# Group D's score matmuls: a head's two sets in turn instead of one after the other

## The reference, cut to what matters

```python
# differential_attention; q, k: (tokens, HEADS=4, 2, DIFF_DH=32)
s = jnp.einsum('bqhtd,bkhtd->bhtqk', q, k).astype(jnp.float32) * scale
p = softmax_f32(s)                              # one softmax for t = 0, one for t = 1
a = (p[:, :, 0] - lam * p[:, :, 1]).astype(v.dtype)
o = jnp.einsum('bhqk,bkhd->bqhd', a, v)
return rmsnorm(o, norm_g) * (1.0 - lam_init)
```

## Time and profile before

| what | value |
|---|---|
| median of 3 runs | 2510.54 us (2506.34 to 2522.1) |
| the profiled execution, first to last instruction | 2507.8 us |
| PE busy with matmuls | 2270.5 us (91%) |
| DVE, ACT, POOL busy | 1359.4 (54%), 790.3 (32%), 493.5 (20%) us |
| group D's attention of layer 0 | 713.4 to 857.8 us |
| group D's attention of layer 1 | 1990.1 to 2104.4 us |

### The profile page before, as it was taken

How to read it: one execution, slowest core, us unless ns; L and a number is a source line. 1 busy time by engine, 2 the same in 40 slices (tenths; PEclk the granted TensorE clock), 3 DMA queues, 4 the chain that set the end, 5 groups by cost and what they waited for, 6 DMA issues and landing times.

```text
span 2507.8 us, 27503 instructions
## 1 busy us (share of the span) xinstructions
PE 2270.5 (91%) x10428; PEld 1820.7 (73%) x10428; DVE 1359.4 (54%) x2448; ACT 790.3 (32%) x1376; POOL 493.5 (20%) x217
## 2 busy tenths in 40 slices
PE   5797989899989779999999989798899997899997
PEld 4675867377866568888888867677466775788886
DVE  5756676244777577676767444554243475411222
ACT  1234242323234442131212233333322344422332
POOL 2200202000200012233222221112001200344442
PEclk9867958555975599999999988777757856899998
DMA  5310302000210013333333211101001100223222
GB/s 202 119 44 16 104 1 94 1 0 1 88 47 1 9 42 134 118 118 118 118 120 126 91 68 34 37 26 61 1 0 39 47 1 17 70 99 101 93 98 70
DMA packets 44770, 161.47 MB, mean 64 GB/s; under 512 B 5344, under 2 KB 5728, under 8 KB 44512
## 3 DMA queue, kind: packets, MB, share of 16 engines
q1 hardware_dynamic: 44640, 159.72, 18.6%
HBM read 157.60 MB, written 2.10 MB: 64 GB/s over the span
## 4 chain that ended last, share of the span: by engine, by line
PE 79%; DVE 11%; ACT 5%; issue 4%; DMA 1%; SPq 0%; POOL 0%; DVEq 0%; ACTq 0%
PE big L1189 64%; PE ob L1189 7%; PE tb L1296 5%; PE tb L1189 3%; DVE pt L908 2%; DVE col L1102 2%; ACT pt L741 1%; DVE pb L952 1%; DMA raw<-w_ada_dram 1%; ACT pb L862 1%; DVE pb L982 1%; DVE h_lo L915 1%; DVE pb L1120 1%; ACT arena L741 1%; DVE z L938 0%
## 5 line engine op out<-in xcount | busy, mean ns | idle before, releaser
L714 POOL TENSOR_TENSOR w_lo<-raw,w_hi 128x1024 fp32r<-128x1024 f32 x182 | 451.8, 2483 | 1244.0 <-ACT w_hi L757 1243.9
L1189 PE MATMUL big<-arena 64*128 64x256 f32 (+4 forms) x1296 | 415.1, 482 | 22.3 <-DVE arena L908 13.4
L1189 PE MATMUL big<-h_hi,w_hi 128*128 128x512 f32 (+1 forms) x1320 | 392.8, 360 | 28.3 <-DVE h_lo L915 27.4
L1189 PE MATMUL big<-h_lo,w_hi 128*128 128x512 f32 (+1 forms) x1320 | 385.5, 354 | 0.0
L1189 PE MATMUL big<-h_hi,w_lo 128*128 128x512 f32 (+1 forms) x1320 | 384.5, 353 | 0.0
L1189 PE MATMUL big<-arena,w_hi 128*128 128x512 f32 (+1 forms) x1536 | 377.1, 354 | 0.0
L1189 PEld LDWEIGHTS big<-arena 64*128 64x128 f32 (+1 forms) x1296 | 278.5, 283 | 124.9 <-issue 71.2
L757 ACT ACTIVATE w_hi<-raw 128x1024 fp32r<-128x1024 f32 x182 | 191.9, 1054 | 420.9 <-PE big L1189 175.8
L1173 DVE SCALAR_TENSOR_TENSOR x<-big,ada,x 128x512 f32<-128x512 f32 x192 | 121.0, 659 | 318.6 <-PE big L1189 254.2
L1189 PEld LDWEIGHTS big<-arena,w_hi 128*128 128x128 f32 x1536 | 251.2, 188 | 41.9
L1189 PEld LDWEIGHTS big<-h_hi,w_hi 128*128 128x128 f32 x1320 | 217.8, 192 | 72.9 <-DVE h_lo L915 31.7
(11 more groups left out here) (118 smaller groups left out, 2097.4 us busy)
## 6 DMA issues: line engine op xcount, KB each, us to landing
raw<-w_ada_dram SPq DMA_DIRECT2D x96, 512.0 KB, 4.4
raw<-w_up_dram SPq DMA_DIRECT2D x64, 512.0 KB, 3.2
raw<-w_down_dram SPq DMA_DIRECT2D x64, 512.0 KB, 3.3
raw<-w_in_dram SPq DMA_DIRECT2D x38, 512.0 KB, 3.5
raw<-w_out_dram SPq DMA_DIRECT2D x16, 512.0 KB, 3.3
gs<-rpb_dram SPq DMA_DIRECT2D x8, 512.0 KB, 3.7
x<-xt_dram SPq DMA_DIRECT2D x1, 3072.0 KB, 12.8
rt<-rope_dram SPq DMA_DIRECT2D x4, 512.0 KB, 3.7
```

The lines of the kernel that those rows point to most:

```text
L714: pool.tensor_tensor(w_lo[:, sl, :], raw[:, b.n % RAW, :], as32(w_hi[:, sl, :]), ALU.subtract).then_inc(split_done, 1)
L1189: return pe.matmul(dst, lhs, rhs, start=start, stop=stop)
```

## The change

PE's `attn` gets a helper for group D. At an even unit it first waits for the free buffers of both units of the pair, and then issues the matmuls of the two sets in turn: first product of set 0, first product of set 1, second of set 0, and so on. At an odd unit it issues no scores. For a local pair that is twelve matmuls in alternation, where before six of one unit and six of the next stood at different places of the loop, with the transposes of an earlier pair between them. The number, shapes and operands of the matmuls stay the same, as do all instructions of the other engines, their order and their semaphores. Groups A, B and C keep their loop.

```diff
+            def both_scores(u0, u1):
+                for u in (u0, u1):
+                    if u.su >= 2:
+                        pe.wait_ge(*big_free(u.su))
+                q = slice(u0.qt * P, (u0.qt + 1) * P)
+                parts = [(S, S + C, S)] + ([(S - u0.wl, S, u0.loc[0] * P)] if u0.loc else [])
+                for at, (a, b, k0) in enumerate(parts):
+                    for n, (qp, kp) in enumerate(((0, 0), (1, 0), (0, 1))):
+                        for u in (u0, u1):
+                            (qs, ks, r), = operands("D", u.h, u.t)
+                            ins = mm(big[u.su % 2][:, a:b], qk(qs, qp)[r, q], qk(ks, kp)[r, k0:k0 + b - a], n == 0, n == 2)
+                            if n == 2 and at == len(parts) - 1:
+                                ins.then_inc(big_ready, 1)
+
             def attn(s):
                 pe.wait_ge(lo_done, s.qlo)
                 for i in range(len(s.units) + LAG + 1):
-                    if i < len(s.units):
+                    if i < len(s.units) and s.g == "D":
+                        if s.units[i].t == 0:
+                            both_scores(s.units[i], s.units[i + 1])
+                    elif i < len(s.units):
```

## The result

The changed kernel takes 2588.36 us (median of 4 runs, 2588.06 to 2593.31), beside 2516.32 us before (4 runs, 2506.34 to 2526.97): ratio 1.030, 95% interval 1.0259 to 1.0341. It is slower, by nearly the forecast amount.

The account below looks back on a forecast made before the run. The prediction took PE as the bound, kept busy in group D by two independently freed score buffers. Span 2507.8 us plus 34 (layer 1) and 46 (layer 0), with medians 2.7 above the span, gave 2590 us, range 2558 to 2632.

Parts of the forecast that it names:

- The bound of the stage: Group D's attention: PE hardly stops, because an even unit may start before the former odd unit's exponential; the change removes this.
- Alternation, 2.4 us a pair: Local pair's scores on PE: twelve alternating matmuls take 2.4 us, between 2.3 (one set) and 4.5 (no overlap).
- The double wait, 8.05 and 10.25 us: Cold local pair, start to next pair: 8.05 us without values, 10.25 with; block 18.3 us against 14.15, +4.15.
- Layer 1: Group D of layer 1: eight blocks, each 4.5 us longer, less about 2 us for the first pairs: +34 us.
- Layer 0: Group D of layer 0: four heads of 47.0 us, each +11.7, less 1 for the first: +46 us.
- The sum: Whole kernel: span 2507.8 us plus 34 and 46 gives 2588; medians lie 2.7 us above, so 2590 us, +3.2%.
- rival 1: Group D: double wait hidden, PE's saving shows, block 10.6 us, total 2451 us; needs a wait under 2.0 us per pair; 6%.
- rival 2: Local and context pairs: alternating sets do not overlap, a pair takes 4.5 us, 74 us more, total 2664 us; 8%.
- rival 3: Group D: denser matmuls keep TensorE at 2.4 GHz, block 14.9 us, total 2535 us; 3%.
- Rival 4: Whole kernel within 1%: overlap gained and wait nearly cancel, total near 2520 us; 3%.

Follow-up runs that it names:

- the reordered kernels: Changed kernel with transposes, copies, scaling and `lo_sub` moved ahead on PE, ACT and DVE; scores alternating or six and six: ratios 0.9917 and 0.9886, on a second measurement both 0.9906.

## Why the prediction was right

*The bound of the stage.* Right. PE idles and the block is longer, at equal clock, although PE's matmul time fell by 52 us in group D. The forecast read in the old trace that the even unit starts ahead of the odd unit's exponential and said that losing this is the cost; the double wait alone, with nothing else changed, reproduced the loss.

*Alternation, 2.4 us a pair.* Slightly mis-sized: 2.29 us, the lower bound. The twelve weight loads cost nothing. The next work starts after 2.22 us.

*The double wait, 8.05 and 10.25 us.* Measured in the block above: 7.96 us (2119.70 to 2127.66) and, from the rest of the 18.27 us, 10.31. The terms of the 7.96 us: scores there after 2.29 us (forecast 2.32), from the even to the odd maximum 3.37 (3.45), maximum to exponential 1.17 (1.17), exponential and sum 0.99 (1.00), then 0.14 to PE (0.05). The forecast took the `lo_sub` to its end, but the next maximum starts 0.09 us before that end; this and the hand-over to PE, 0.09 too short, cancel. The forecast's own terms add up to 7.99 and not to the 8.05 that it wrote, since 0.03 us was added twice without a source; it does no harm. The 2.4 us taken for the pair is not in this sum, because DVE only needs the even unit's scores.

*Layer 1.* First and last of seven values matmuls after, as in the earlier trace rows:

```profile
2062.30 2.93 PE L1189 MATMUL ob<-pt,arena 128*128 128x256 f32 x12 [2.04 <-DVE pt L908]
...
2170.01 2.93 PE L1189 MATMUL ob<-pt,arena 128*128 128x256 f32 x12 [2.04 <-DVE pt L908]
```

107.71 us for six blocks, 17.95 each: 18.3 less the 0.35 allowed for warm spells. The warm spells were not spread evenly: two blocks took 17.31 us at a clock of 0.60, the other four 18.27. That half of the old gain would be left was an estimate, so its exact size is partly luck. The stage grew by 32.0 us, forecast 34; by these blocks the deduction for its two ends should have been 4 us, not 2.

*Layer 0.* Values of the context job, one head apart, as in the earlier trace rows:

```profile
761.75 1.19 PE L1189 MATMUL ob<-pt,arena 128*128 128x256 f32 x4 [2.34 <-DVE pb L1124]
...
807.31 1.19 PE L1189 MATMUL ob<-pt,arena 128*128 128x256 f32 x4 [2.34 <-DVE pb L1124]
...
853.85 1.19 PE L1189 MATMUL ob<-pt,arena 128*128 128x256 f32 x4 [2.34 <-DVE pb L1124]
```

45.56 us (clock 0.54) and 46.54 us (clock 0.50), forecast 47.0. Six pairs in a row in the trace, from 802.07 to 848.60, take 8.02, 7.96, 10.31, 5.27, 8.13 and 6.84 us from one start to the next, where the forecast has, in this order, 7.9, 8.05, 10.25, 5.3, 8.1 and 7.4. So the half microsecond a head is in one term, the first pair behind the context pairs (7.4). The stage grew by 43.0 us, forecast 46. Four times the half microsecond is 2 us of the 3; the rest is about what the one warmer head gained, for which the forecast allowed nothing.

*The sum.* Group D came to +75.0 where +80 was forecast, both layers a little too high. The profiled span is 2586.7 us against 2587.8, closer than that because the rest of the span happened to be 3.9 us longer in this execution. The medians moved by 72.0 us, from 2516.3, while the forecast started from the 2510.5 of the first three runs. So the closeness of 2588.4 to 2590 is luck; that group D grew by about 80 is not.

*The rivals.* The faster one (rival 1) fell: its deciding point was a wait under 2.0 us a pair, and PE waits 4.21 us for the exponential in a pair without values and 1.58 + 2.04 us in one with values. Its picture of a hidden double wait comes true only in the reordered kernels, with 12.1 us a block where it had 10.6. No overlap (rival 2) is excluded by 2.29 us against 4.18 on the same rows. The clock (rival 3) fell a little, 0.55 to 0.52 and 0.57 to 0.54, and did not rise. Rival 4 fell with rivals 1 and 3. In the range, "half the way to the clock case" would be 28 us down and not 32; the result does not hang on it.

## What to carry to other kernels

Two buffers that come free one by one let an engine work ahead; a step that takes both at once waits for the later one, and all that stands in queue order ahead of that release goes on the chain. Before merging two steps, follow the later buffer's release back through every queue and count what is ahead of it (here 3.45 us of DVE work and a copy that waits for PE itself). If they are merged, move the work that the wait holds back in front of it, on all engines together: DVE and ACT in the new order with PE in its old one took 35 us more than the kernel before, with PE's order changed as well it was 20 to 27 us less.

## What the runs showed of the hardware

Matmuls on different 32 rows of the array overlap without any alternation in the program: two sets of six, issued one after the other, took 2.86 us together, 4.18 us on the same rows, 2.29 us in alternation. The Trainium skill, page "TensorE: Matmul & The Clock Gate", Part 3, says that matmuls keep strict program order in start and end. The 2.86 us contradict it for starts: with the second set behind the first's sixth matmul the row would be, by estimate from the earlier trace rows, at least 1.7 + 2.3 = 4.0 us. The records agree: in that row a 512-column matmul starts at 2116.03 and two 256-column ones after it, at 2116.21 and 2116.42, though the program has all three 512-column matmuls of the first set ahead of the second set. So the written order that the text assumes for every engine does not hold in full for PE's matmuls. Of the ends no run here shows anything, since the profile models them. The page's other sentence, that tiles on different row groups run together for one duration, agrees to the resolution of the trace (2.29 us for six and for twelve).
